# A transformer stack on one core: a quarter of the weight split of the mixers goes to GpSimd

## The reference, cut to what matters

```python
def second_block(x, ...):
    for l in range(2):
        x = x + 0.5 * rms_norm(swiglu(rms_norm(x), w1, w3, w2))      # feed-forward
        x = x + rms_norm(mixer_block(rms_norm(x), w_in, ...))        # the mixer
        x = x + rms_norm(cross_attention(...))
        x = x + 0.5 * rms_norm(swiglu(...))                          # feed-forward

def mixer_block(h, ...):
    u = h @ w_in                                  # 1024 x 9216: conv, q, k, v, pool, gates
    y_conv = conv_branch(u_conv, ...)             # glu, 31-tap causal depthwise conv, layer norm, @ conv_pw
    y_attn = diff_attention(q, k, v, ...) @ attn_o    # 8 heads, two softmax maps each
    y_pool = pool_branch(u_pool, ...)             # windowed means, @ pool_w, @ pool_o
    merged = g0 * y_conv + g1 * y_attn + g2 * y_pool  # g: sigmoids of the gate columns of u
    return merged @ w_out
```

## Time and profile before

| | us |
|---|---|
| median of three runs | 2324.55 (2321.91 to 2325.38) |
| the profiled execution, its own time | 2317.8 |
| its span, first to last instruction | 2316.0 |
| PE busy | 2202.4 (95%) |
| DVE busy | 1700.5 (73%) |
| ACT busy | 1190.2 (51%) |
| POOL busy | 96.9 (4%) |

### The profile page before, as it was taken

The page is one execution under the profiler, slowest core; times in us unless marked ns, Lnnn a source line. Parts: engine busy times, 40 slices in busy tenths (PEclk is TensorE's granted clock), DMA queues, the critical chain, the costliest instruction groups (busy, mean ns, idle before and its releaser), DMA issues.

```text
span 2316.0 us, 43919 instructions
## 1 busy us (share of the span) xinstructions
PE 2202.4 (95%) x18003; PEld 2137.2 (92%) x18003; DVE 1700.5 (73%) x2712; ACT 1190.2 (51%) x1867; POOL 96.9 (4%) x93
## 2 busy tenths in 40 slices
PE   6988899999999999889999999999999889999998
PEld 5977899999999998889998999999998789998998
DVE  7666887997675798887655765765798888656764
ACT  2565445774544544555544544544544555635453
POOL 1000000110010000000000010010000000000110
PEclk7998899999999999999999999999999999999999
DMA  8735575668566754445453766565763346463764
GB/s 240 211 117 167 160 253 175 196 192 251 164 206 189 220 184 130 124 144 175 155 183 110 210 195 191 174 206 186 220 191 118 122 147 186 151 187 113 211 182 133
DMA packets 407256, 409.34 MB, mean 177 GB/s; under 512 B 18319, under 2 KB 400689, under 8 KB 407058
## 3 DMA queue, kind: packets, MB, share of 16 engines
q1 hardware_dynamic: 396033, 389.20, 55.1%
q0 software_dynamic: 11024, 17.34, 2.9%
HBM read 405.37 MB, written 1.12 MB: 176 GB/s over the span
## 4 chain that ended last, share of the span: by engine, by line
PE 66%; DVE 23%; ACT 6%; issue 4%; DMA 1%; SPq 0%; DVEq 0%; POOL 0%; ACTq 0%; POOLq 0%
PE gemm_ps L976 44%; PE gemm_ps L979 16%; DVE weights_lo L1627 7%; DVE x_res L2100 6%; DVE mod_partial L1732 1%; ACT weights_hi L1240 1%; ACT e L1421 1%; DVE neg_max L1860 1%; DVE h_lo L1772 1%; PE misc_ps L1157 1%; PE misc_ps L1120 1%; DVE y L1808 1%; PE gemm_ps L959 0%; PE misc_ps L1140 0%; DMA raw_weights<-in_w_in_dram 0%
## 5 line engine op out<-in xcount | busy, mean ns | idle before, releaser
L1627 DVE TENSOR_TENSOR weights_lo<-raw_weights,weights_hi 128x1024 fp32r<-128x1024 f32 x704 | 835.3, 1198 | 361.4 <-ACT weights_hi L1240 358.0
L1240 ACT CAST weights_hi<-raw_weights 128x1024 fp32r<-128x1024 f32 x704 | 717.3, 1032 | 598.3 <-PE gemm_ps L976 423.2
L976 PE MATMUL gemm_ps<-h_hi,weights_hi 128*128 128x256 f32 x3280 | 928.7, 283 | 18.5 <-DVE h_lo L1762 5.9
L976 PE MATMUL gemm_ps<-h_lo,weights_hi 128*128 128x256 f32 x3280 | 913.2, 278 | 0.0
L976 PE MATMUL gemm_ps<-h_hi,weights_lo 128*128 128x256 f32 x3280 | 913.1, 278 | 0.0
L976 PEld LDWEIGHTS gemm_ps<-h_hi,weights_hi 128*128 128x128 f32 x3280 | 621.1, 189 | 28.4 <-issue 19.9
L976 PEld LDWEIGHTS gemm_ps<-h_lo,weights_hi 128*128 128x128 f32 x3280 | 621.3, 189 | 3.0 <-issue 2.7
L976 PEld LDWEIGHTS gemm_ps<-h_hi,weights_lo 128*128 128x128 f32 x3280 | 620.9, 189 | 0.0
L2100 DVE SCALAR_TENSOR_TENSOR x_res<-zp,param_cols,x_res 128x256 f32<-128x256 f32 x480 | 196.6, 477 | 0.0
L979 PE MATMUL gemm_ps<-weights_hi,hidh 128*128 128x256 f32 x688 | 189.9, 276 | 0.0
L979 PE MATMUL gemm_ps<-weights_hi,hidl 128*128 128x256 f32 x688 | 189.9, 276 | 0.0
(11 more groups left out here) (341 smaller groups left out, 3074.7 us busy)
## 6 DMA issues: line engine op xcount, KB each, us to landing
raw_weights<-in_ffn_w_dram SPq DMA_DIRECT2D x256, 512.0 KB, 4.4
raw_weights<-in_w_in_dram SPq DMA_DIRECT2D x200, 512.0 KB, 4.0
raw_weights<-in_w_mod_dram SPq DMA_DIRECT2D x48, 512.0 KB, 4.9
raw_weights<-in_w_up_dram SPq DMA_DIRECT2D x44, 512.0 KB, 4.7
raw_weights<-in_xattn_kv_dram SPq DMA_DIRECT2D x32, 512.0 KB, 4.4
raw_weights<-in_w_out_dram SPq DMA_DIRECT2D x24, 512.0 KB, 4.5
raw_weights<-in_w_down_dram SPq DMA_DIRECT2D x20, 512.0 KB, 5.0
raw_weights<-in_w_branch_dram SPq DMA_DIRECT2D x16, 512.0 KB, 4.6
```

What stands on the lines that cost most here:

```text
L976: mm = pe.matmul(ps[:, c, 0:T], w[:, m, kt, c * P:(c + 1) * P], x[:, f, :], start=start, stop=stop_)
L1240: act.copy(unit_of(WH, m % SPLIT, u), unit_of(RAWB, u["raw"] % RAW, u)).then_inc(sems["weights_rounded"], 1)
L1627: dve.tensor_tensor(unit_of(WL, m % SPLIT, u), unit_of(RAWB, u["raw"] % RAW, u), unit_of(WH, m % SPLIT, u), ALU.subtract).then_inc(sems["w ...
```

## The change

GpSimd subtracts the last of the four blocks of a unit (128x256), DVE only the first three (128x768), for units that are marked `shared`. A second semaphore, `weights_rest_pool`, tells of GpSimd's part; PE waits for both before the unit, and SP waits for both before it fetches into the raw buffer again.

```diff
@@ plan / mixer
         enter(key, f"norm{l}", 16)
+        shared_from = len(units)
         add("pads2", l=l, hid_unit=readers["HID"])
...
         S.extend(spread(main + last[:half], conv(range(0, NF, 2))))
+        for kind, u in S:
+            if kind == "unit" and u["n"] >= shared_from:
+                u["shared"] = u["cols"] == COLS and u["nkt"] == UNIT_KT
@@ block.sync
                 sp.wait_ge(*done(("free", r - RAW)))
+                if raws[r - RAW].get("shared"):
+                    sp.wait_ge(sems["weights_rest_pool"], at("rest_pool", raws[r - RAW]["m"]))
@@ pe_unit
             pe.wait_ge(sems["weights_rest"], at("rest", u["m"]))
+            if u.get("shared"):
+                pe.wait_ge(sems["weights_rest_pool"], at("rest_pool", u["m"]))
@@ block.vector, lo
-            dve.tensor_tensor(unit_of(WL, m % SPLIT, u), unit_of(RAWB, u["raw"] % RAW, u), unit_of(WH, m % SPLIT, u), ALU.subtract).then_inc(sems["weights_rest"], 1)
+            mine = slice(0, UNIT_KT - 1 if u.get("shared") else None)
+            dve.tensor_tensor(unit_of(WL, m % SPLIT, u)[:, mine], unit_of(RAWB, u["raw"] % RAW, u)[:, mine], unit_of(WH, m % SPLIT, u)[:, mine], ALU.subtract).then_inc(sems["weights_rest"], 1)
@@ block.gpsimd
+        def rest(m):
+            if m >= len(splits) or not splits[m].get("shared"):
+                return
+            u = splits[m]
+            pool.wait_ge(sems["weights_rounded"], at("rounded", m))
+            kt = UNIT_KT - 1
+            pool.tensor_tensor(WL[:, m % SPLIT, kt, :], RAWB[:, u["raw"] % RAW, kt, :], WH[:, m % SPLIT, kt, :], ALU.subtract).then_inc(sems["weights_rest_pool"], 1)
+            up("weights_rest_pool", ("rest_pool", m))
...
         for kind, k in steps:
+            if kind == "unit":
+                rest(k["m"] + AHEAD)
```

More of the change, by code:

```diff
@@ L687, in build @@
         "consts_in", "ident_in", "x_in", "bias_in", "small_in", "windows_in", "hankel_in", "gain_in", "line_out", "flip_in", "hankel_late_in", "mem_in", "rows_in", "blocks_in", "y_out",
-        "weights_rounded", "weights_rest", "gemm_done", "act_drain", "vec_drain", "act_norm", "vec_norm", "pe_norm",
+        "weights_rounded", "weights_rest", "weights_rest_pool", "gemm_done", "act_drain", "vec_drain", "act_norm", "vec_norm", "pe_norm",
         "act_attn", "vec_attn", "pe_attn", "act_rnn", "vec_rnn", "pe_rnn", "act_ffn", "vec_ffn", "act_split",
```

## The result

The changed kernel takes **2339.39 us** (median of 10 runs, 2332.70 to 2342.24), the kernel before beside it 2323.65 (10 runs, 2318.30 to 2331.49). The ratio is 1.0061, with a 95% interval of 1.0047 to 1.0075: slower by 15.7 us on the medians. The profiled execution has a span of 2337.9 us, 21.9 more than before's 2316.0.

What follows compares the result with a forecast made beforehand. DVE was taken to have no air beside a full PE from 785 to 887 us. Per mixer +6.4, 0, +1.5 and +0.3 make 8.2 us, 16.4 for both: 2324.55 + 16.4 = 2341 us, range 2316 to 2360.

Steps and rivals of the forecast that it cites:

- Who leads: First mixer, 785 to 887 us: PE and DVE both full, DVE idles only 1.1 us, so its lateness reaches PE nearly whole.
- That DVE stands still while POOL reads: A DVE instruction with both tensors in SBUF blocks while POOL reads SBUF; four taps took 2.73 us instead of 1.67.
- The stall of 0.53 us: DVE's predicted loss per POOL subtraction of 256 elements, half the 1.06 us seen at 512; likely 0.4 to 0.75 us.
- the bound: Limits on DVE's loss per POOL subtraction: nothing if DVE always reads PSUM, 1.06 us if it doesn't shrink with size.
- The share of 0.925 in which it is paid: 785 to 887 us: subtractions and taps, needing two SBUF tensors, are 92.2 of DVE's 99.7 us; 0.49 us cost per unit.
- The stage 785 to 887, +6.4 us: 34 shared units at 0.22 us net make 7.5 us per mixer; DVE's 1.1 us of idling take up a part.
- From 937 on, +1.5 us: 937 to 1005 us: 15 shared units at 0.10 us net, with a 0.70 share of two-SBUF work, per mixer.
- From 887 to 937, nothing: Four shared units cost 0 because DVE has 10 us of room; without that cover 0.9 us.
- The sum, 8.2 us a mixer: Total predicted loss over a mixer's stages, including +0.3 us for seven other units; 16.4 us for both mixers.
- Fetches and waits at nothing: PE's and SP's second waits and the later bias and window fetches cost nothing; the fetches have some 20 us of room.
- POOL starving: Rival, chance 0.05: POOL gets in only when DVE pauses, PE stands; +27 us in each mixer, above 2350 us.
- The signs named ahead: New profile: DVE's subtraction mean above 1.1 us, taps' mean from 476 to above 500 ns, POOL's subtractions 0.7 to 0.9 us.

## Why the prediction was right

- **Who leads.** That DVE has no air from 785 to 887 us was right: two thirds of the loss come from the first 34 units, and sparing DVE the same work there without a stall shortens the mixer.
- **That DVE stands still while POOL reads.** Shown: subtraction, copy and memset in POOL's place order themselves as it says, and only the memset leaves the taps alone.
- **The stall of 0.53 us**, taken as half of 1.06, measured 0.48. That it goes with the size is shown by the 1.04 us of two blocks. Neither end of the bound was near.
- **The share of 0.925 in which it is paid** was too high. In the first stage the taps lost 10.0 us, `zp` 4 x (851 - 692) = 0.6 (692 ns was its median before) and the subtractions 34 x (1028 - 954) = 2.5, with 954 as the undisturbed mean of the kernel without POOL's part. That is 13.1 us for 34 units, 0.39 each, 0.8 of a stall and not 0.925. A reason shows at 817.65: POOL's instruction was passed over until DVE read PSUM, so such instructions get more of POOL's work than their share of the time. That this is all of it was only argued. Net of the 0.27 spared, a unit costs DVE 0.12 us here and not 0.22.
- **The stage 785 to 887, +6.4 us**, measured +5.0 in the trace, 4.2 a mixer by the ratios (half of 8.3). 34 x 0.12 = 4.1 is what DVE's rows give.
- **From 937 on, +1.5 us.** DVE's groups of the changed kernel from 945 to 1013 us:

```profile
L2109 DVE SCALAR_TENSOR_TENSOR x_res<-zp,param_cols,x_res 128x256 f32<-128x256 f32 x60 | 29.4, 554 | 0.0
...
L1636 DVE TENSOR_TENSOR weights_lo<-raw_weights,weights_hi 128x768 fp32r<-128x768 f32 x15 | 14.2, 955 | 0.1
```

60 x (554 - 476) = 4.7 us for 15 units are 0.31 each, where 0.37 was predicted: net +0.04 and so 0.7 us. The 26 units behind the first stage cost 2.0 us a mixer by their own run, with 887 to 937 in it.
- **From 887 to 937, nothing.** This term was wrong. DVE had the room, and what the four shared units cost it there was taken up; but the stage begins with PE waiting for the exponentials, the lateness brought along from the first stage made that wait 2.25 us, and behind it the clock fell. The fall cost 1.4 us in each mixer of the trace. The prediction had looked at the clock only from 937 us on, and only as something that a faster kernel might win.
- **The sum, 8.2 us a mixer**, measured 7.1 and 8.1 between the marks; 16.4 in all against 15.7 on the medians. The first stage was put 1.4 us too high, and what lies behind it, 1.8, came out at 2.1 (7.1 - 5.0), of which 1.4 are the clock and 0.7 the rest. That the sum is nearer than its terms is luck: without the clock's 1.4 us the loss was 5.7 and 6.7 us, so the stalls were overrated by 2.5 and 1.5 us, and what was left out filled the gap.
- **Fetches and waits at nothing**: shown for the waits by the run with memsets, and for the fetches by the run with early ones together with the trace.
- **POOL starving.** Its premise was seen in part: POOL does get in late, up to 2.77 us for an instruction of 0.73. It was not paid, since PE comes to the unit three units, some 8 us, later.
- **The signs named ahead.** The taps' mean above 500 ns came (564). The subtraction's mean above 1.1 us did not (1028), since the stall falls on the taps more often than their share: they lost 10.0 of 13.1 us. POOL's median is 0.92 us, a little above the range of 0.7 to 0.9 given.

## What to carry to other kernels

Before handing a part of DVE's elementwise work to GpSimd, look at what DVE does beside it: if that has two SBUF tensors, the price is DVE's stall, here 0.48 us for a subtraction that spared 0.27. Look for a place in the trace where the two already run together, price it there, and multiply by the share of DVE's time with such instructions. In both stages here that came out too high (0.49 against 0.39 us, 0.37 against 0.31). Then ask which waits of TensorE the lateness will lengthen, and what clock it is granted behind them. Where both engines are full, less is given back than is taken: the same 32 us of DVE's work were worth 14 us when taken away from the kernel before, and 27 when taken away from the one that was late.

## What the runs showed of the hardware that was not expected

POOL can be passed over. With DVE's instructions back to back, a POOL instruction that takes 0.73 us beside a DVE instruction on PSUM took up to 2.77, and it did not always slip in behind the DVE instruction that was running when it began.

PE has two paces at the full granted clock. The timeline of before shows it, with starts of matmuls 15 apart in one unit and in another, and the clock of both stretches behind them:

```profile
863.01 0.28 PE L979 MATMUL gemm_ps<-weights_hi,h_lo 128*128 128x256 f32 x1
...
864.78 0.28 PE L979 MATMUL gemm_ps<-weights_hi,h_lo 128*128 128x256 f32 x1
...
872.91 0.28 PE L976 MATMUL gemm_ps<-h_hi,weights_lo 128*128 128x256 f32 x1
...
874.62 0.28 PE L976 MATMUL gemm_ps<-h_hi,weights_lo 128*128 128x256 f32 x1
```
```profile
861.00:865.00 4.00, 4.00 (x36) 4.00 (x35) 4.00 (x8) 1.55 (x3) 0.00 (x0) 1.00 0.46 147
871.00:875.00 4.00, 4.00 (x38) 4.00 (x37) 4.00 (x9) 1.98 (x2) 0.00 (x0) 1.00 0.74 234
```

Fifteen matmuls take 1.77 us in the first stretch and 1.71 in the second, 0.118 and 0.114 us each, and PE is busy without a gap in both. For a unit of 24 that is some 0.1 us; a pace stays for tens of units, so it can move an execution by several us. I found no rule for when it changes, and no run was made for it.
